# Moving every SBUF buffer behind the activation parts by 352 bytes in a hybrid attention layer

## The chip, the cores and the metric

The kernel runs on one core of a Trainium2 chip. The metric is the device time of the program in microseconds. The engines are named as in the profile: PE is TensorE's matmul stream and PEld its weight loads, DVE is VectorE, ACT is ScalarE, POOL is GpSimd, SP is SyncE, which issues nearly all DMAs.

## What is computed

One decoder layer on a sequence of 256 tokens with 4096 channels, in float32:

```python
h = rms_norm(x, pre_norm_w)
proj = h @ w_in                       # 4096 x 15408: queries, keys, values, gates
oa = nsa_mixer(...)                   # 16 heads: compressed, selected and window branches
ob = dilated_mixer(...)               # 16 heads: three (window, dilation) patterns merged
mix = concat([oa * silu(za), ob * silu(zb)])
x = x + rms_norm(mix @ w_out, post_norm_w)   # w_out: 4096 x 4096
```

Nearly all of the arithmetic is in the two large products with `w_in` and `w_out`. Attention over 256 tokens is small beside them.

## The kernel before, in words

**Precision.** A float32 product is made from three single-pass products. Each operand is split into a high part, which is the value rounded to the format that TensorE reads in one pass (fp32r), and a low part, which is the rest. The kernel sums hi·hi, hi·lo and lo·hi.

**Chunks and pairs.** The weights are worked through in 38 chunks of 512 columns by the helper `gemm_pair` (and one chunk of the compression weights and a narrow one of gate columns, which are handled apart at L810 and L821). A chunk has 32 blocks of 128 rows, taken two at a time as 16 pairs. For a pair, SP brings 128 x 2 x 512 float32 values into one of four slots of `raw` (`load_pair`, L384). ACT writes the high part to `w_parts[:, 0]` (`split`, L929), DVE subtracts it from `raw` and writes the low part to `w_parts[:, 1]` (L1239). PE then runs 12 matmuls: for each of the two row blocks and each of the two token tiles, L640 (stationary activation hi, moving weight hi), L643 (activation hi, weight lo) and L646 (activation lo, weight hi). The stationary operand is 128 columns of `x_parts` (512 bytes in each partition); the moving operand is 512 columns of `w_parts` (2048 bytes). The count is 38 x 16 x 12 = 7296 such matmuls, the last chunk's held pairs among them.

**Order.** Each engine's program is written out by hand. Attention, rotations, softmax and transposes are placed at fixed steps between the pairs of the large products, so that PE always has a pair ready. The semaphores `hi_ready`, `lo_ready` and `weights_used` tie ACT, DVE, PE and SP together through four slots.

**Placement in SBUF.** `build` has a bump allocator: `at` is the next free byte offset in each partition, `sb` rounds sizes up to 32 bytes, and a buffer may be given an explicit `offset` to share bytes with an earlier one. Such offsets are all worked out from buffers of the same list (`region`, `late`, `v_off` and so on). The first buffer is `x_parts` (65536 bytes a partition), the activation parts. All others come behind it. Worked out from the list, the byte offsets that matter are:

| buffer | role in the matmuls | offset before | modulo 64 | offset after | modulo 64 |
|---|---|---|---|---|---|
| x_parts | stationary of L640, L643, L646; moving of L810 | 1152 | 0 | 1152 | 0 |
| raw | landing place of weight DMAs | 99456 | 0 | 99808 | 32 |
| w_parts | moving of L640, L643, L646, L821 | 115840 | 0 | 116192 | 32 |
| b_q_hi, b_k_hi | L674 stationary, moving | 164992, 152704 | 0 | +352 | 32 |
| b_pt_hi | moving of L689, L691 | 181376 | 0 | +352 | 32 |
| vc (also b_v_hi) | stationary of L718, L689, L690 | 213536 | 32 | 213888 | 0 |
| w2_sb | stationary of L853 | 214560 | 32 | 214912 | 0 |
| pc_t (also b_pt_lo) | moving of L718, L690 | 215584 | 32 | 215936 | 0 |

Blocks and slots inside these buffers step by multiples of 512 bytes, so one remainder holds for all of a buffer. `x_parts`, `w_parts` and nearly all large buffers start at 1152 modulo 2048 before the change.

Of the kernel before, what the change touches and what calls it, by code (L numbers as in the profile page):

```python
# [111 lines left out]
def build(nc, x, x_t, positions, norm_cols, consts, w_in, w1, w2, post_w, w_out, out):  # L112

    ctx = ExitStack()
    with ctx:
        at = [1152]

        def sb(name, shape, dt=F32, offset=None):
            size = 4 * math.prod(shape[1:])
            where = at[0] if offset is None else offset  # L120
            if offset is None:
                at[0] += (size + 31) // 32 * 32
            t = nc.alloc_sbuf_tensor_at(name, shape, dt, offset=where)
            return t, where
# [2 lines left out]
        x_parts, _ = sb("x_parts", [P, KB, 2, SEQ], F32R)  # L127
        x_hi, x_lo = x_parts[:, :, 0, :], x_parts[:, :, 1, :]

        mix_t, region = sb("mix_t", [P, KB, SEQ])  # L130
        xt_raw, _ = sb("xt_raw", [P, KB, SEQ], offset=region)
        flat, _ = sb("flat", [P, CMP_LEN, 2, 2, GROUPS * CMP_PAD], F32R, offset=region)
# [1689 lines left out]
```

## Time and profile before

| | |
|---|---|
| Median of 2 runs | 1766.16 us (1765.94 and 1766.38) |
| Span of the profiled execution | 1763.9 us, first to last instruction; its own device time is not listed apart, the two runs' times stand 2.0 to 2.5 us above this span |
| PE busy | 1757.8 us, 7902 matmul records |
| PE weight loads | 1456.4 us |
| DVE, ACT, POOL busy | 1153.4, 886.8, 598.9 us |
| DMA | 344.77 MB, mean 195 GB/s |

Matmuls are pipelined: a record lasts some 0.39 us, but the next one starts about 0.23 us after it. So the busy time of PE is a union of overlapping records, and what counts for the pace is the distance from start to start, which is read from the order in time. Rows of that view give starts in us with two decimals.

### The profile page before, as it was taken

The page shows a single profiled execution, that of the slowest core. Times are in us where ns is not written, and L with a number is a line of the kernel's source. Part 1 is how long each engine was busy: PE and PEld are TensorE (multiplying, and loading weights), DVE is VectorE, ACT ScalarE, POOL GpSimd, SP SyncE. Part 2 cuts the span into 40 slices and gives each one's busy share as a digit, 9 for nine tenths or more (in the row PEclk, how much of TensorE's full clock was granted, in tenths as well). Part 3 has the DMA queues.
Part 4 walks back from the last instruction along what each step waited for, and adds up shares of the span by engine and source line. Part 5 has one row for each costly group of instructions (what it writes and reads, how often), then busy time and mean ns, then how long its engine had stood idle before and what let it go on. Part 6 is the DMA issues. An engine that isn't in the chain of part 4 may idle for free.

```text
span 1763.9 us, 22877 instructions
## 1 busy us (share of the span) xinstructions
PE 1757.8 (100%) x7902; PEld 1456.4 (83%) x7902; DVE 1153.4 (65%) x1192; ACT 886.8 (50%) x1216; POOL 598.9 (34%) x834
## 2 busy tenths in 40 slices
PE   9999999999999999999999999999999999999998
PEld 7888888888888888888888888888888888888886
DVE  7657656787888878656665666566655784444445
ACT  7643455464554545456435643564456554444443
POOL 3335303367593948721353034304431510000000
PEclk9999999999999999999999999999999999999999
DMA  9866687656565656666666666666666656667665
GB/s 294 254 199 188 188 248 229 179 161 185 157 189 151 185 160 174 183 197 182 179 195 196 182 181 197 194 190 176 191 194 191 190 185 217 213 213 212 213 202 204
DMA packets 184267, 344.77 MB, mean 195 GB/s; under 512 B 15216, under 2 KB 19568, under 8 KB 184176
## 3 DMA queue, kind: packets, MB, share of 16 engines
q1 hardware_dynamic: 183456, 342.58, 66.2%
q8 instruction: 62, 1.02, 0.2%
q10 hardware_dynamic: 720, 0.93, 0.1%
q14 instruction: 29, 0.24, 0.0%
HBM read 339.27 MB, written 4.19 MB: 195 GB/s over the span
## 4 chain that ended last, share of the span: by engine, by line
PE 99%; DMA 0%; ACT 0%; SPq 0%; DVE 0%; ACTq 0%; issue 0%
PE acc L640 31%; PE acc L646 31%; PE acc L643 31%; PE acc L821 1%; PE scores L810 0%; PE scores L709 0%; DMA raw<-in_w_in 0%; PE scores L742 0%; PE scores L741 0%; PE scores L740 0%; PE heads L757 0%; PE heads L758 0%; PE heads L759 0%; PE scores L665 0%; PE heads L692 0%; PE trans L657 0%
## 5 line engine op out<-in xcount | busy, mean ns | idle before, releaser
L1239 DVE TENSOR_TENSOR w_parts<-raw,w_parts 128x1024 fp32r<-128x1024 f32 x620 | 784.4, 1266 | 556.9 <-ACT w_parts L929 555.3
L929 ACT ACTIVATE w_parts<-raw 128x1024 fp32r<-128x1024 f32 x620 | 656.2, 1059 | 662.6 <-PE acc L646 649.6
L640 PE MATMUL acc<-w_parts,x_parts 128*128 128x512 f32 x2424 | 946.7, 391 | 0.2 <-DVE w_parts L1239 0.2
L646 PE MATMUL acc<-w_parts,x_parts 128*128 128x512 f32 x2424 | 943.8, 389 | 0.0
L643 PE MATMUL acc<-w_parts,x_parts 128*128 128x512 f32 x2424 | 943.3, 389 | 0.0
L646 PEld LDWEIGHTS acc<-w_parts,x_parts 128*128 128x128 f32 x2424 | 455.1, 188 | 95.8 <-DVE x_parts L1281 0.3
L640 PEld LDWEIGHTS acc<-w_parts,x_parts 128*128 128x128 f32 x2424 | 455.3, 188 | 93.4 <-issue 0.6
L643 PEld LDWEIGHTS acc<-w_parts,x_parts 128*128 128x128 f32 x2424 | 455.3, 188 | 93.0
L515 POOL COPY rot<-tok_b 32x256 f32<-32x256 f32 x120 | 86.9, 724 | 140.6 <-DVE tok_b L1613 135.7
L499 POOL TENSOR_TENSOR rot<-tok_a,trig 128x512 f32<-128x512 f32 x18 | 30.6, 1699 | 260.5 <-ACT tok_a L935 121.4
L515 POOL COPY b_first_t<-probs 32x128 f32<-32x128 f32 x64 | 31.1, 485 | 163.1 <-DVE probs L1686 160.6
L1603 DVE RECIPROCAL mixed<-mixed 128x256 f32<-128x256 f32 x32 | 55.8, 1745 | 0.4
L515 POOL COPY b_later_t<-probs 32x256 f32<-32x256 f32 x64 | 49.2, 769 | 19.1 <-DVE probs L1686 16.6
L949 ACT ACTIVATE probs<-probs,negmax 128x128 f32<-128x128 f32 (+1 forms) x80 | 34.7, 435 | 32.0 <-DVE negmax L1480 32.0
L483 POOL TENSOR_TENSOR rot<-rot,tok_a 128x512 f32<-128x512 f32 x15 | 27.6, 1842 | 55.5 <-ACT tok_a L968 55.2
L515 POOL COPY rot<-probs 32x256 f32<-32x256 f32 x64 | 40.5, 632 | 17.3 <-DVE probs L1520 14.8
L581 POOL CAST pc_t<-rows_c 32x128 fp32r<-32x128 f32 x64 | 27.7, 432 | 32.9 <-DVE rows_c L1577 30.3
L515 POOL COPY tok_a<-probs_more 32x128 f32<-32x128 f32 x64 | 35.9, 560 | 2.7
L515 POOL COPY k_t<-tok_a 32x256 f32<-32x256 f32 x32 | 20.0, 624 | 43.7 <-DVE tok_a L1348 42.5
L515 POOL COPY tok_a<-probs 32x128 f32<-32x128 f32 x64 | 33.8, 527 | 2.7
L515 POOL COPY k_t<-rot 32x256 f32<-32x256 f32 x32 | 28.4, 888 | 17.5 <-DVE rot L1458 8.6
L515 POOL COPY qraw_t<-probs_more 32x128 f32<-32x128 f32 x64 | 31.8, 497 | 2.7
(240 smaller groups left out, 1010.1 us busy)
## 6 DMA issues: line engine op xcount, KB each, us to landing
raw<-in_w_in SPq DMA_DIRECT2D x478, 512.0 KB, 3.7
raw<-in_w_out SPq DMA_DIRECT2D x128, 512.0 KB, 4.3
raw<-in_w SPq DMA_DIRECT2D x16, 512.0 KB, 4.7
x_tok<-in_x SPq DMA_DIRECT2D x16, 256.0 KB, 5.3
xt_raw<-in_x_t SPq DMA_DIRECT2D x7, 512.0 KB, 6.2
wpost<-in_post_w SPq DMA_DIRECT2D x8, 256.0 KB, 5.1
out<-y SPq DMA_DIRECT2D x3, 512.0 KB, 2.8
out<-y SPq DMA_DIRECT2D x5, 256.0 KB, 2.1
```

The costliest lines, as they stand in the source:

```text
L483: nc.gpsimd.tensor_tensor(square_sum, square_sum, squares[n % 2], ALU.add).then_inc(squares_added, 1)
L499: nc.gpsimd.tensor_tensor(r4, s4, cos, ALU.mult).then_inc(rope_muls, 1)
L515: last = nc.gpsimd.tensor_copy(dst[cols, :, :, rows], src[rows, :, :, cols])
L581: last = nc.gpsimd.tensor_copy(pc_t[cols, :, :, b * QUARTER // PART_ROWS, rows], src[rows, :, :, cols])
L640: nc.tensor.matmul(o, stat_hi, mov_hi, start=(k == 0), stop=False)
L643: nc.tensor.matmul(o, stat_hi, mov_lo, start=False, stop=False)
L646: last = nc.tensor.matmul(o, stat_lo, mov_hi, start=False, stop=(k == KB - 1))
L821: last = nc.tensor.matmul(acc[:, 1, v, :], flat[:, k, v, :, :], w_parts[:, :, at % SPLIT_SLOTS, k % 2, CMP_HIDDEN * v:CMP_HIDDEN * (v + 1) ...
L929: nc.scalar.activation(w_hi[:, n % SPLIT_SLOTS, :, 0:width], raw[:, n % RAW_SLOTS, :, 0:width], ACT.Copy).then_inc(hi_ready, 1)
L949: last = nc.scalar.activation(p, p, ACT.Exp, bias=negmax[:, slot % 4, i:i + 1], accum_out=den[:, slot % 4, i:i + 1])
L1239: V.tensor_tensor(w_lo[:, s, :, 0:width], raw[:, n % RAW_SLOTS, :, 0:width], w_hi[:, s, :, 0:width].bitcast(F32), ALU.subtract).then_inc(l ...
L1603: V.reciprocal(half, half).then_inc(silu_step, 1)
```

## The change

One line is added in `build`, behind the allocation of `x_parts` and ahead of all others:

```diff
         x_parts, _ = sb("x_parts", [P, KB, 2, SEQ], F32R)
         x_hi, x_lo = x_parts[:, :, 0, :], x_parts[:, :, 1, :]
 
+        at[0] += 352
         mix_t, region = sb("mix_t", [P, KB, SEQ])
         xt_raw, _ = sb("xt_raw", [P, KB, SEQ], offset=region)
```

`x_parts` stays at 1152. Every later buffer, those with explicit offsets included, moves up by 352 bytes = 5 x 64 + 32 in each partition. Nothing overlaps that did not before, and the list still ends inside SBUF. No instruction, wait, shape or order differs. Between two buffers behind `x_parts` the distance stays as it was; between `x_parts` and any other it grows by 352.

## Rows read from the trace of the kernel before

**Rows 1.** The page: span, busy time by engine, granted clock, DMA queue.
```profile
span 1763.9 us, 22877 instructions
PE 1757.8 (100%) x7902; PEld 1456.4 (83%) x7902; DVE 1153.4 (65%) x1192; ACT 886.8 (50%) x1216; POOL 598.9 (34%) x834
...
PEclk9999999999999999999999999999999999999999
...
q1 hardware_dynamic: 183456, 342.58, 66.2%
```

**Rows 2.** The page: the chain that ended last, by engine.
```profile
PE 99%; DMA 0%; ACT 0%; SPq 0%; DVE 0%; ACTq 0%; issue 0%
```

**Rows 3.** Waits of PE: line, releaser, us in total, times, longest.
```profile
PE scores L777 <- DVE stat L1317: 1.2, 1, 1.2
PE acc L640 <- DVE w_parts L1239: 0.2, 1, 0.2
```

**Rows 4.** The page's costliest groups: the split and the three products.
```profile
L1239 DVE TENSOR_TENSOR w_parts<-raw,w_parts 128x1024 fp32r<-128x1024 f32 x620 | 784.4, 1266 | 556.9 <-ACT w_parts L929 555.3
L929 ACT ACTIVATE w_parts<-raw 128x1024 fp32r<-128x1024 f32 x620 | 656.2, 1059 | 662.6 <-PE acc L646 649.6
...
L640 PEld LDWEIGHTS acc<-w_parts,x_parts 128*128 128x128 f32 x2424 | 455.3, 188 | 93.4 <-issue 0.6
```

**Rows 5.** Order in time, PE, 1420 to 1464 us: start, us, instruction; first and last.
```profile
1419.74 0.39 PE L646 MATMUL acc<-w_parts,x_parts 128*128 128x512 f32 x1
...
1463.94 0.39 PE L646 MATMUL acc<-w_parts,x_parts 128*128 128x512 f32 x1
```

**Rows 6.** Order in time, PE, the last product records and those after them.
```profile
1753.85 1.88 PE L908 MATMUL heads<-x_tok,cst 128*128 128x512 f32 x4
1755.56 1.02 PE L908 MATMUL scores<-x_tok,cst 128*128 128x512 f32 x2
```

**Rows 7.** Order in time, PE, around the first L718.
```profile
374.22 0.39 PE L643 MATMUL acc<-w_parts,x_parts 128*128 128x512 f32 x1
374.45 0.40 PE L646 MATMUL acc<-w_parts,x_parts 128*128 128x512 f32 x1
374.69 0.63 PE L718 MATMUL heads<-pc_t,vc 128*128 128x256 f32 x4
375.16 0.39 PE L640 MATMUL acc<-w_parts,x_parts 128*128 128x512 f32 x1
```

**Rows 8.** Order in time, PE, around the first L689.
```profile
863.69 0.40 PE L646 MATMUL acc<-w_parts,x_parts 128*128 128x512 f32 x1
863.93 0.28 PE L689 MATMUL heads<-b_pt_hi,b_v_hi 128*128 128x256 f32 x1
```

**Rows 9.** Order in time, PE, L853.
```profile
312.09 0.40 PE L646 MATMUL acc<-w_parts,x_parts 128*128 128x512 f32 x1
312.33 0.55 PE L853 MATMUL trans<-gelu,w_sb 128*128 128x64 f32 x4
```

**Rows 10.** Order in time, PE, around L674 to L676.
```profile
829.57 0.39 PE L646 MATMUL acc<-w_parts,x_parts 128*128 128x512 f32 x1
829.80 0.28 PE L674 MATMUL scores<-b_k_hi,b_q_hi 128*128 128x256 f32 x1
829.91 0.28 PE L675 MATMUL scores<-b_k_lo,b_q_hi 128*128 128x256 f32 x1
830.03 0.28 PE L676 MATMUL scores<-b_k_hi,b_q_lo 128*128 128x256 f32 x1
...
830.51 0.40 PE L640 MATMUL acc<-w_parts,x_parts 128*128 128x512 f32 x1
...
831.90 0.39 PE L640 MATMUL acc<-w_parts,x_parts 128*128 128x512 f32 x1
```

**Rows 11.** Stretches: PE, PEld, DVE, ACT, POOL busy; PEclk, DMA share, GB/s.
```profile
0.00:50.00 50.00, 48.59 (x205) 39.51 (x206) 37.01 (x48) 35.01 (x53) 15.99 (x13) 1.00 0.90 294
1420.00:1750.00 330.00, 330.00 (x1458) 273.34 (x1457) 170.45 (x161) 143.15 (x165) 7.22 (x8) 1.00 0.66 205
```

**Rows 12.** Waits of SP's queue: line, releaser, us in total, times, longest.
```profile
SPq L384 <- DVE w_parts L1239: 1248.0, 554, 5.1
```

## The prediction

> **What bounds the kernel.** I read the page first. PE is busy over the whole span at the full clock (2.4 GHz), the other engines are busy 65% of it or less, and the weight queue takes 66% of the DMA engines' time [rows 1]. The chain that ended last is PE for 99% [rows 2]. Then the waits of PE: 1.2 us at the very start and 0.2 us for a split, nothing else [rows 3]. So the kernel is one unbroken string of matmuls, and its time is their number times the distance between their starts. That distance comes from the order in time: in a stretch with nothing but the three products there are 195 distances between 1419.74 and 1463.94, 44.20 us, so 226.7 ns each [rows 5]. All but a few per cent of the time is this: 7296 x 0.2267 = 1654 us of the 1764.
>
> **What is inside 226.7 ns.** 512 columns at 2.4 GHz are 213.3 ns, or 512 periods; 226.7 ns are 544. So 32 periods (13.3 ns) are lost at each matmul. They aren't the plain cost of one matmul after another: the L908 records, which take two periods for each of 512 columns, follow each other at (1755.56 - 1753.85) / 4 = 427.5 ns, that is 1026 periods for 1024 [rows 6]. A weight load is running beside each product, recorded at 188 ns [rows 4]. I read the loss as the two reads of PE, 512 bytes of stationary and 2048 of moving operand in each partition, getting in each other's way or in step with something, at the addresses of the two. Those addresses are all that the change touches.
>
> **The change, part by part.** No instruction is added, dropped or moved, and no wait. Three things could respond to an address.
>
> (a) The products. 7296 matmuls (L640, L643, L646) and the 32 of L810 have one operand in `x_parts` and one behind it: 7328 whose two starts were equal modulo 64 before and differ by 32 after. All others keep their relation, both operands being moved. No row shows the new relation in a long string, so I bound it. The nearest rows are places where a product at the usual pace is followed by a matmul whose stationary operand starts at 32 modulo 64 while the moving one is at 0. L646 to L718 takes 374.69 - 374.45 = 0.24 us, L646 to L689 0.24, L646 to L853 0.24 [rows 7, 8, 9]; over the four L718 and eight L689 blocks it is 0.237. The control has all operands at 0 modulo 64: L646 to L674 takes 0.23 us [rows 10]. So the first distance at the new relation is longer by 10 ns. If it stayed so, 7328 x 10 ns = +73 us. That is the upper end. The control also shows how the pace behaves once it is disturbed: the six distances after the L674 block sum to 831.90 - 830.51 = 1.39 us, 231.7 ns each, before 226.7 comes back [rows 10]. A string that never settles would cost 5 ns a matmul, +37 us.
>
> The lower end: with the loss gone, a matmul would take 512 periods and the 2 of L908, 214.2 ns, -12.5 ns each and -92 us. I don't expect all of that, since nothing in the trace at 512 columns comes near it. The moving operand at 32 modulo 64 is seen only in L718 and L690, with 256 columns: four L718 in 375.16 - 374.69 = 0.47 us, 117.5 ns each [rows 7], where the aligned L674 to L676 take 0.12 (829.91 to 830.03) [rows 10]. That is no penalty for the moving operand's own offset, and 2.5 ns in its favour. It speaks against me; but there both operands are at 32, so their relation is the old one.
>
> The value that I take: the settled paces are whole multiples of 16 periods, 544 = 34 x 16 for 512 columns [rows 5] and 288 = 18 x 16 for 256 columns (0.12 us) [rows 10]. The pace seems to lock to such a step. One step more is 560 periods, 233.3 ns, which lies between 231.7 and 237. So +6.7 ns x 7328 = **+48.9 us**.
>
> (b) The splits and the small work. ACT's and DVE's halves of a split, 1059 and 1266 ns [rows 4], read and write at 32 modulo 64 instead of 0. A pair lasts 12 x 226.7 = 2720 ns on PE, and DVE is busy 52% of the long stretch [rows 11]. I price this at nothing: PE hides it, and DVE's split could last 2.1 times as long before PE waited. If that cover were gone, each ns over 2720 would count 620 times.
>
> (c) The DMAs. 183,456 packets of the weight queue land at another remainder. SP's queue waits 1248 us for slots to come free [rows 12], so it is early nearly everywhere. The exception is the start, where the DMA share is 0.90 and PE already loses 1.4 us of 50 [rows 11]. A few per cent more for each packet would cost up to 50 x 0.04 = 2 us there; I take 0. Between the ends (nothing, 2 us) the long stretch is nearer, with a share of 0.66 [rows 11].
> The Trainium skill (DMA: Bandwidth & Descriptors, "How a descriptor splits into AXI transactions") speaks against the change here: a descriptor that starts off a 256-byte boundary pays for the bytes below its start. By that, an estimate for 2048 bytes in beats of 32: from 128 modulo 256 before 68 beats, from 224 after 71, or 4% more. No row shows it; the sum would be the 2 us higher.
>
> **Sum.** 1766.2 + 48.9 + 0 + 0 = **1815 us**. The sum is made against the profiled execution (span 1763.9, so 1812.8 after); the runs stand 2.0 to 2.5 us above that span, and I add to their median.
>
> **Rivals.**
> *Same pace (1766 us).* The relation of the two addresses doesn't matter, or the stream settles to 544 periods again after a few disturbed matmuls, as it does after every disturbance in the trace [rows 10]. For it: the return to 226.7 is complete each time. Against it: the three 0.24 distances [rows 7, 8, 9] need a reason, and the stationary operand's own remainder would be one; that doesn't change for the products. 27%.
> The Trainium skill (SBUF — State Buffer, "Who interferes with whom") gives this result: PE has two independent read ports and never waits for anyone. The trace agrees with its companion number only in part: the page TensorE: Matmul & The Clock Gate ("Back-to-back issue gap") has 512 columns at about 216 ns, and here it is 226.7.
>
> *Faster (about 1717 us).* The mechanism sits in PE's reads during the weight load, at every product: with the starts 32 bytes apart the two reads stay clear of each other more of the time, and the lock falls one step lower, to 528 periods, 220.0 ns. 7328 x -6.7 ns = -48.9 us, 1717. With the loss gone but for what the L908 rows leave it would be 1674. It decides the sign as soon as the settled distance is under 226.7, and passes 2% (35 us) at 4.8 ns, 221.9 ns. For it: the 32 lost periods, and the 2.5 ns at L718. Against it: the first distances at the new relation are longer, not shorter. 31%, 17 of it at 528 periods or just above, 14 lower than that.
>
> *Slower, as forecast.* 42%: 560 periods or a string that doesn't settle (1803 to 1816) 27%, up to the full 10 ns (1839) 13%, beyond it 2%.
>
> That the change doesn't do what it says is no case: all offsets go through one counter.
>
> **How the numbers follow.** 2% is about what a measurement of this kernel can tell from no change. The forecast is the likeliest case, 1815, whose own range is 1800 to 1840. The case of no change and the faster one hold more than half together, so the range takes them in: down to 1705, which leaves out the 14% of a pace below 220 ns for the most part, and up to 1842, which leaves out 2%. Slower by over 2% (above 1801) 0.41, within 2% 0.28, faster 0.31.
>
> **What would show it.** In the changed kernel's order in time, the distance between two products over a long string: 233 ns if right, 226.7 for no change, 220 or less for the faster case. L674 to L676, whose operands both moved, should stay at 0.12 us. L646 to L718, whose stationary operand comes to 0 modulo 64 while the moving one goes to 32, should lie near the new pace. The waits of PE should stay under 3 us; if they grow instead, (b) or (c) was wrong. The DMA share should stay near 0.66 for the same bytes in each us. I am wrong at (a), the taken value, if the string settles on the other side, and wrong on the premise if the pace is 226.7 throughout.

## The result: slower by 2.7%

The changed kernel takes 1813.39 us (1813.30 and 1813.48) where the one before takes 1766.16; the ratio is 1.0268 with a 95% interval of 1.0250 to 1.0286. The profiled execution has a span of 1811.2 us, 47.3 more than before [rows 1].

In the changed kernel all line numbers behind the new line are one higher: L641, L644 and L647 are the three products that were L640, L643 and L646. Its page: span, busy time, the products' groups and the weight loads'.

```profile
span 1811.2 us, 22877 instructions
PE 1805.3 (100%) x7902; PEld 1456.9 (80%) x7902; DVE 1150.3 (64%) x1192; ACT 888.3 (49%) x1216; POOL 588.4 (32%) x834
...
PEclk9999999999999999999999999999999999999999
...
q1 hardware_dynamic: 183456, 342.58, 64.6%
...
L1240 DVE TENSOR_TENSOR w_parts<-raw,w_parts 128x1024 fp32r<-128x1024 f32 x620 | 780.7, 1260 | 605.4 <-ACT w_parts L930 603.5
...
L647 PE MATMUL acc<-w_parts,x_parts 128*128 128x512 f32 x2424 | 960.1, 396 | 0.0
L644 PE MATMUL acc<-w_parts,x_parts 128*128 128x512 f32 x2424 | 958.3, 395 | 0.0
L641 PE MATMUL acc<-w_parts,x_parts 128*128 128x512 f32 x2424 | 957.0, 395 | 0.0
L644 PEld LDWEIGHTS acc<-w_parts,x_parts 128*128 128x128 f32 x2424 | 455.2, 188 | 110.8
```

As many matmuls at the same full clock. A weight load still lasts 188 ns and a DVE split even 6 ns less than before [rows 4]; only the product records are longer, 395 or 396 ns where the page before has 389 to 391. PE's one wait, and the wait of SP's queue for free slots:

```profile
PE scores L778 <- DVE stat L1318: 1.2, 1, 1.2
```

```profile
SPq L385 <- DVE w_parts L1240: 1290.8, 556, 5.2
```

PE waits for nothing new [rows 3], and SP waits 43 us longer for slots [rows 12], as is to be expected where PE frees them later. The stretch at the start and a long one near the end, columns as in [rows 11]:

```profile
0.00:50.00 50.00, 48.78 (x199) 39.22 (x200) 35.37 (x48) 34.60 (x53) 14.31 (x12) 1.00 0.89 288
1460.00:1790.00 330.00, 330.00 (x1416) 265.47 (x1415) 164.58 (x151) 140.75 (x160) 7.20 (x8) 1.00 0.66 203
```

A stretch of 330 us now holds 1416 matmul starts instead of 1458. The DMA share is 0.66 as before, and at the start 0.89 instead of 0.90. The order in time on PE shows where the time is:

```profile
1459.77 0.39 PE L644 MATMUL acc<-w_parts,x_parts 128*128 128x512 f32 x1
1460.00 0.40 PE L647 MATMUL acc<-w_parts,x_parts 128*128 128x512 f32 x1
1460.23 0.39 PE L641 MATMUL acc<-w_parts,x_parts 128*128 128x512 f32 x1
1460.46 0.39 PE L644 MATMUL acc<-w_parts,x_parts 128*128 128x512 f32 x1
1460.70 0.40 PE L647 MATMUL acc<-w_parts,x_parts 128*128 128x512 f32 x1
...
1503.87 0.39 PE L644 MATMUL acc<-w_parts,x_parts 128*128 128x512 f32 x1
```

189 distances in 1503.87 - 1459.77 = 44.10 us: 233.3 ns each, 560 periods, where it was 226.7 and 544 [rows 5]. They aren't even. In the trace's nanoseconds three of them repeat as 231, 231, 238, together 700 ns, or 1680 periods; before, every one in such a stretch was 226 or 227.

### The profile page after: what moved, and what is told of

It is laid out like the page before. It is cut to its first block, busy times and chain, and to the rows that moved or that the text cites. A ratio compares the mean times of both kernels' runs of the same rounds, so it can differ in the third digit from the quotient of the medians.

```text
span 1811.2 us, 22877 instructions
## 1 busy us (share of the span) xinstructions
PE 1805.3 (100%) x7902; PEld 1456.9 (80%) x7902; DVE 1150.3 (64%) x1192; ACT 888.3 (49%) x1216; POOL 588.4 (32%) x834
## 3 DMA queue, kind: packets, MB, share of 16 engines
q1 hardware_dynamic: 183456, 342.58, 64.6%
## 4 chain that ended last, share of the span: by engine, by line
PE 100%; ACT 0%; ACTq 0%; issue 0%; DVE 0%
PE acc L647 31%; PE acc L644 31%; PE acc L641 31%; PE acc L822 1%; PE scores L811 0%; PE scores L710 0%; PE scores L741 0%; PE heads L758 0%; PE scores L743 0%; PE scores L742 0%; PE heads L759 0%; PE heads L760 0%; PE scores L778 0%; PE scores L666 0%; PE heads L693 0%; PE trans L658 0%
## 5 line engine op out<-in xcount | busy, mean ns | idle before, releaser
L647 PE MATMUL acc<-w_parts,x_parts 128*128 128x512 f32 x2424 | 960.1, 396 | 0.0
L644 PE MATMUL acc<-w_parts,x_parts 128*128 128x512 f32 x2424 | 958.3, 395 | 0.0
L641 PE MATMUL acc<-w_parts,x_parts 128*128 128x512 f32 x2424 | 957.0, 395 | 0.0
L644 PEld LDWEIGHTS acc<-w_parts,x_parts 128*128 128x128 f32 x2424 | 455.2, 188 | 110.8
L641 PEld LDWEIGHTS acc<-w_parts,x_parts 128*128 128x128 f32 x2424 | 455.3, 188 | 108.8
L647 PEld LDWEIGHTS acc<-w_parts,x_parts 128*128 128x128 f32 x2424 | 455.0, 188 | 107.8
L551 POOL TENSOR_TENSOR rot<-qraw_t,turn_t 128x512 f32<-128x512 f32 x8 | 14.2, 1780 | 60.5 <-ACT qraw_t L942 60.5
```

What stands on the lines that cost most here:

```text
L641: nc.tensor.matmul(o, stat_hi, mov_hi, start=(k == 0), stop=False)
L644: nc.tensor.matmul(o, stat_hi, mov_lo, start=False, stop=False)
L647: last = nc.tensor.matmul(o, stat_lo, mov_hi, start=False, stop=(k == KB - 1))
```

## The experiments

In the table, the shift is the distance in bytes that is added between the starts of stationary and moving operand of the products (moving less stationary), and the periods are the mean distance of two starts in a long undisturbed stretch, in ns, times 2.4, which gives periods of the full clock. Where a kernel adds lines of its own, the products' line numbers move with them: L642, L645 and L648 are the three products in e4, e7, e8 and e12.

| kernel | shift | modulo 256 | us | ratio to before (95%) | periods a product |
|---|---|---|---|---|---|
| before | 0 | 0 | 1766.2 | | 544.0 |
| after | 352 | 96 | 1813.4 | 1.0268 (1.0250 to 1.0286) | 560.0 |
| e1_shift_64 | 64 | 64 | 1782.1 | 1.0090 (1.0061 to 1.0119) | 549.3 |
| e2_all_352 | 0 | 0 | 1766.4 | 1.0000 (0.9989 to 1.0011) | 544.0 |
| e3_stat_32 | 32, see below | 32 | 1811.9 | 1.0258 (1.0229 to 1.0288) | 560.0 |
| e4_wparts_352 | 352 | 96 | 1813.3 | 1.0267 (1.0237 to 1.0296) | 560.0 |
| e5_shift_128 | 128 | 128 | 1806.2 | 1.0229 (1.0185 to 1.0273) | 557.7 |
| e6_shift_96 | 96 | 96 | 1813.2 | 1.0268 (1.0224 to 1.0312) | 560.0 |
| e7_inner_16 | 16 | 16 | 1800.8 | 1.0198 (1.0154 to 1.0242) | 556.0 |
| e8_inner_4 | 4 | 4 | 1842.1 | 1.0432 (1.0387 to 1.0477) | 570.0 |
| e9_shift_256 | 256 | 0 | 1766.2 | 1.0000 (0.9988 to 1.0011) | 544.0 |
| e10_shift_192 | 192 | 192 | 1812.6 | 1.0263 (1.0234 to 1.0293) | 560.0 |

**Is it the relation of the two operands, or where the moving one lies?** Two kernels part these. One moves everything, the activation parts too, by the same 352 bytes:

```diff
-        at = [1152]
+        at = [1152 + 352]
```

> Everything moved by 352 bytes, the activation parts too, so that the relation of stationary and moving start is that of before and both are at 32 modulo 64. Theory R (the relation of the two starts sets the pace): 1766 us, 226.7 ns. Theory M (the moving operand's own remainder modulo 64 sets it): 1813 us, 233.3 ns on average. If both operands' remainders add: up to 1840 us.

1766.4 us. The order in time of this kernel is that of before:

```profile
1499.83 0.39 PE L646 MATMUL acc<-w_parts,x_parts 128*128 128x512 f32 x1
1500.06 0.39 PE L640 MATMUL acc<-w_parts,x_parts 128*128 128x512 f32 x1
...
1501.87 0.39 PE L646 MATMUL acc<-w_parts,x_parts 128*128 128x512 f32 x1
```

Nine distances in 2.04 us are 226.7 ns, with moving and stationary operand of the products at 32 modulo 64. Moving all buffers alike by these 352 bytes costs nothing. The other kernel moves the activation parts by 32 bytes and all others by 64:

```diff
-        at = [1152]
+        at = [1152 + 32]
...
+        at[0] += 32
         mix_t, region = sb("mix_t", [P, KB, SEQ])
```

> Only the activation parts moved, by 32 bytes; all others land at 0 modulo 64 (moved by 64). Theory R: the starts differ by 32 modulo 64, 1813 us. Theory M: 1766 us. The rows of before at L718, L689 and L853 (0.24 us where the stationary operand alone is at 32) speak for a slower pace here, 1800 to 1840 us; if those were only a first disturbance, 1766.

1811.9 us, with `w_parts` and `raw` still at 0 modulo 64. Its shift needs the arithmetic: the parts move by 32, the rest by 64, so moving less stationary grows by 32. The pace is 560 periods too, in another string. Four distances make up its round (about 231, 235, 233 and 234 ns), 1500.73 - 1499.80 = 0.93 us in these lines; in the trace's nanoseconds it is 933.3, or 2240 periods:

```profile
1499.80 0.40 PE L641 MATMUL acc<-w_parts,x_parts 128*128 128x512 f32 x1
...
1500.73 0.40 PE L644 MATMUL acc<-w_parts,x_parts 128*128 128x512 f32 x1
```

Theory R, the relation of the two starts, holds and theory M, the moving operand's own remainder, falls in both runs.

**Is PE alone in it?** `w_parts` alone goes to the new remainder. `raw`, into which the DMAs write, stays where it was; the buffers behind `w_parts` move by 384 bytes, which leaves their remainder modulo 64 (modulo 256 they move by 128):

```diff
+        at[0] += 352
         w_parts, _ = sb("w_parts", [P, 2, SPLIT_SLOTS, 2, NC], F32R)
+        at[0] += 32
```

> Only w_parts at 32 modulo 64 (moved by 352); raw, mix_t and all other buffers at 0. PE reads w_parts, ACT and DVE write it, no DMA touches it. Theories R and M, the reads of PE: 1813 us and the uneven string of 231, 231 and 238 ns. If the DMAs into raw or the other buffers had a part in the slowdown: less than that, down to 1766.

1813.3 us, all of the loss, in the string 231, 231, 238; nine distances in 2.10 us:

```profile
1499.79 0.39 PE L645 MATMUL acc<-w_parts,x_parts 128*128 128x512 f32 x1
...
1501.89 0.39 PE L645 MATMUL acc<-w_parts,x_parts 128*128 128x512 f32 x1
```

The landing place of the DMAs has no part in the loss, since `raw` didn't move. The buffers behind `w_parts` did, but the kernel with everything moved has them elsewhere too and loses nothing.

ACT and DVE write `w_parts` while PE reads the activation parts, so their writes stand at the same new distance, and no run here stops them. The trace of the changed kernel speaks against them. From 1470 to 1740 us every three successive distances sum to 699 or 700 ns, over 1158 starts, while DVE and ACT are busy for half of the time and less (164.58 and 140.75 of 330 us in the stretch above). A loss that came from their writes would be there during a split and gone between two.

**Which distances count as the same?** Each of these kernels changes only the number in the line that the change adds.

> Every buffer behind the activation parts moved by 64 bytes instead of 352. If only the starts modulo 64 count: distance 226.7 ns, 1766 us. If the two operands' distance in bytes counts beyond 64 (a period of 128 or more): a pace between 222 and 237 ns, 1730 to 1840 us. If the splits or DMAs were behind the slowdown through their remainder modulo 64: also 1766 us, so this run does not tell that one apart.

1782.1 us: neither as before nor as after. So the remainder modulo 64, on which the prediction rested, isn't the whole of it. The order in time of this kernel:

```profile
1499.67 0.39 PE L647 MATMUL acc<-w_parts,x_parts 128*128 128x512 f32 x1
...
1501.73 0.39 PE L647 MATMUL acc<-w_parts,x_parts 128*128 128x512 f32 x1
```

Nine distances in 2.06 us: three rounds of 686.7 ns or 1648 periods (226, 229, 232 ns).

> Every buffer behind the activation parts moved by 128 bytes. The run at 64 gave 1782 us, so the relation counts beyond 64 bytes. Period 128: 226.7 ns and 1766 us, as before. Period 256 or 512: another pace, 1740 to 1840 us.

> Moved by 96 bytes, which is 352 less two times 128. Period 128: 1813 us and the same string 231, 231, 238 ns as after the change. Period 256: also 1813, since 352 is 96 modulo 256. Period 512 or longer: another pace.

128 gives 1806.2 us, which excludes a period of 128 bytes. Its round is of seven matmuls, 1626.7 ns or 3904 periods; to two decimals:

```profile
1499.69 0.39 PE L647 MATMUL acc<-w_parts,x_parts 128*128 128x512 f32 x1
...
1501.31 0.39 PE L641 MATMUL acc<-w_parts,x_parts 128*128 128x512 f32 x1
```

96 gives the time of 352, 1813.2 us, down to the string 231, 231, 238.

> Every buffer behind the activation parts moved by 256 bytes. 96 and 352 gave the same time and the same string, 0, 64 and 128 three different ones. If the relation counts modulo 256: 226.7 ns and 1766 us. If it counts modulo 512, and 96 and 352 agree by accident: another pace, 1780 to 1815 us.

1766.2 us and even distances again, as these lines of the kernel moved by 256 bytes show (ten in 2.26 us):

```profile
1499.71 0.39 PE L647 MATMUL acc<-w_parts,x_parts 128*128 128x512 f32 x1
...
1501.97 0.39 PE L641 MATMUL acc<-w_parts,x_parts 128*128 128x512 f32 x1
```

0 and 256 agree, 96 and 352 agree, and 0, 64, 96 and 128 all differ. So the relation counts modulo 256 bytes, as far as these two pairs can show it.

> Moved by 192 bytes, the last multiple of 64 below 256 that is untried. If relation 0 is the best case: over 1775 us. If the loss falls off evenly on both sides of 0, as at 64 (1782 us): about 1782. A faster kernel than before (a pace under 226.7 ns) has a chance of 1 in 8.

1812.6 us, and in the long stretch near the end 560 periods at each single matmul. The loss isn't even on both sides of 0: 64 ahead costs 16 us, 64 behind (192) costs 46. None of the relations tried is faster than 0, which the kernel before has; so no run pointed to a version that beats both.

**Below 32 bytes.** The allocator rounds sizes up to 32 bytes, so `w_parts` was placed inside a buffer that is 64 bytes longer (`e` is 4 elements, then 1); the buffers behind it move by those 64 bytes:

```diff
-        w_parts, _ = sb("w_parts", [P, 2, SPLIT_SLOTS, 2, NC], F32R)
+        w_size = 2 * SPLIT_SLOTS * 2 * NC
+        w_room, _ = sb("w_parts", [P, w_size + 16], F32R)
+        w_parts = w_room[:, e:e + w_size].rearrange("p (a s k n) -> p a s k n", a=2, s=SPLIT_SLOTS, k=2)
```

> Only w_parts moved, by 16 bytes, inside a buffer made 64 bytes longer. If the pace falls with the relation step by step (0 bytes 226.7 ns, 32 or 96 bytes 233.3, 64 bytes 229): 227 to 233 ns, 1770 to 1813 us. If the start inside a 32-byte piece doesn't count: 1766 us. A relation that keeps the two reads apart could be faster: under 1750 us.

> Only w_parts moved, by 4 bytes, one element. If whole lines of 16 or 32 bytes are read and the start inside one doesn't count: 1766 us. If a start off the line costs one more line at each read: some periods a matmul more, 1770 to 1815 us.

1800.8 and 1842.1 us; the second lies above the range that was expected. One element off is the worst case measured: 570 periods a product. In these lines nine distances take 1501.81 - 1499.67 = 2.14 us, 237.8 ns each:

```profile
1499.67 0.40 PE L642 MATMUL acc<-w_parts,x_parts 128*128 128x512 f32 x1
1499.90 0.40 PE L645 MATMUL acc<-w_parts,x_parts 128*128 128x512 f32 x1
1500.14 0.40 PE L648 MATMUL acc<-w_parts,x_parts 128*128 128x512 f32 x1
...
1501.81 0.40 PE L642 MATMUL acc<-w_parts,x_parts 128*128 128x512 f32 x1
```

These two runs can't tell a cost of the relation from one of a start off a 16- or 32-byte boundary; a kernel with both operands off by 4 bytes would, and wasn't run. So the dependence modulo 256 rests on the relations that are multiples of 32.

**Does the loss follow the length of the weight load?** Half of the stationary columns are left out in 30 of 32 row blocks, so half of the tokens get the sums of two row blocks only (the stationary columns are tokens, not output channels as the expectation has it):

```diff
-                        o = acc[:, parity, t, 0:width]
-                        stat_hi, stat_lo = hi[:, k, t * P:(t + 1) * P], lo[:, k, t * P:(t + 1) * P]
+                        m = P if k in (0, KB - 1) else P // 2
+                        o = acc[0:m, parity, t, 0:width]
+                        stat_hi, stat_lo = hi[:, k, t * P:t * P + m], lo[:, k, t * P:t * P + m]
```

> The kernel before with stationary operands of 64 columns instead of 128 in 30 of 32 row blocks, which leaves half of the output channels' sums out; matmuls, moving operands and transfers stay. Theory R says that the 32 periods over 512 are lost while a weight load reads beside the product, so they go with its length: 6840 matmuls lose 16 periods (6.7 ns) less, 1720 us. Rival, that they are a fixed price of a matmul or a start on a grid: 1766 us.

> The same in the changed kernel. Theory R: the 48 periods lost on average go down to 24 in 6840 matmuls, 10 ns each, 1745 us, and the cost of the 352 bytes falls from 47 to about 25 us. If only the start decides, and the length of the load doesn't: the cost of the 352 bytes stays at 47 us.

Both kernels missed what was expected of them. The loads are shorter, as the weight loads of the first of the two show:

```profile
L644 PEld LDWEIGHTS acc<-w_parts,x_parts 128*64 128x64 f32 (+1 forms) x477 | 65.7, 138 | 43.1
```

138 ns instead of 188. But that kernel takes 1786.4 us (ratio 1.0115, 1.0085 to 1.0144), 20 us more than before, at 551.5 periods a product; with the 352 bytes it is 1798.3 us (1.0182, 1.0153 to 1.0212), 15 us less than the changed kernel, at 555.8. Half of the stationary columns made one faster and the other slower. So the loss over 512 periods is not an amount for each byte loaded, as theory R was put there. It isn't a fixed price either, since the rival's 1766 us is excluded as well. What the pair does show is that the cost of the 352 bytes falls from 47 us to 12 when the stationary operand has half of its columns. That shortens the load and also halves the rows of `acc` that a product writes; the operands' addresses, the moving operand and the number of matmuls stay. That it is the load's length which counts, and not the narrower output, is not shown.

## Why the prediction was right

**The bound.** PE's unbroken string was the bound and is the bound after; 1.2 us of waits in all.

**Term (a), the products: right in mechanism, 7% too large in size.** The mechanism was that the distance between the starts of the two operands sets the pace, and the runs show it. 560 periods was the value taken and is the settled pace to a tenth of a period. The term was 48.9 us for 7328 matmuls; the span grew by 47.3. The products' own share of that is smaller. In the trace before, the 7189 distances from one product to the next sum to 1634.9 us, 227.4 each and not 226.7, for the disturbed stretches are in them [rows 10]. After, they sum to 1680.5, so the step is 45.6 us or 6.3 ns. Of the some 3 us that the term was too large, 2.3 are in the 6.3 ns instead of 6.7 and 0.9 in the 139 matmuls of the term that aren't a product with another behind it. The rest of the span's growth is 1.6 us. The first product starts 0.4 us later (6.14 instead of 5.70 us; with everything moved it is 6.15, so this isn't the relation), and 1.2 came from the places between the products' runs, most of it from matmuls that I had put at nothing because both of their operands move. They pay when the uneven string runs into them. The first L758 block of the changed kernel shows it:

```profile
405.47 0.40 PE L758 MATMUL heads<-pt_hi,v_hi 128*128 128x512 f32 x1
405.70 0.40 PE L759 MATMUL heads<-pt_lo,v_hi 128*128 128x512 f32 x1
405.94 0.39 PE L760 MATMUL heads<-pt_hi,v_lo 128*128 128x512 f32 x1
406.17 0.39 PE L641 MATMUL acc<-w_parts,x_parts 128*128 128x512 f32 x1
```

0.70 us for three, where the same three took 0.68 in the trace before:

```profile
395.57 0.39 PE L757 MATMUL heads<-pt_hi,v_hi 128*128 128x512 f32 x1
...
396.25 0.39 PE L640 MATMUL acc<-w_parts,x_parts 128*128 128x512 f32 x1
```

Over all 24 such blocks it is 701.5 ns against 680.0.

**The remainder was the wrong one.** The prediction compared the starts modulo 64. The runs show 256. That the rows still gave the right answer was luck. The relation at L718, L689 and L853 before [rows 7, 8, 9] was not just any odd multiple of 32. Those buffers start at 32 modulo 256 and `w_parts` at 128, so the moving operand was 96 ahead, and 352 is 96 modulo 256. Had the change been 64 bytes, the argument by remainders modulo 64 would have said 1766 us, and the run gave 1782.

**The whole steps of 16 periods** held for whole rounds, not for one matmul at a time. In the long strings of the changed kernel no product takes 560 periods; three take 1680. Rounds of other kernels are whole multiples of 16 too: 1648 for three (64 bytes), 3904 for seven (128 bytes), 2240 for four (32 bytes) and 2224 for four (16 bytes: 227, 234, 235, 230 ns). So "one step more" was a guess that came out: the mean pace is 560 at 32, 96 and 192 bytes, but 549.3, 556.0, 557.7 and 570.0 at 64, 16, 128 and 4, none of which is a whole step. Why 16, no run shows.

**The bounds.** The upper end from the first disturbed distance, +10 ns, was not reached by this relation, though 4 bytes came to it (26 periods or 10.8 ns over 544). The lower end was far off: nothing tried came under 544.

**Terms (b) and (c)** are nothing, as priced: `w_parts` alone gives the whole loss, and the whole set moved by 352 gives none, with each split and each DMA landing at the new remainder. The estimate of 2 us more for the start of a descriptor off a 256-byte boundary, from the Trainium skill (DMA: Bandwidth & Descriptors, "How a descriptor splits into AXI transactions"), isn't borne out: the packets of the weight queue took 64.6% of 1811.2 us, 1170 us, where they took 66.2% of 1763.9 us, 1168 us [rows 1]. With everything moved by 352 it is 66.4% of 1764.4 us, 1172, and with `raw` unmoved (`w_parts` alone) 64.6% of 1811.3 us, 1170; the time with everything moved is 1766.4 us.

**The rival of the same pace** needed another reason for the three 0.24 distances, the stationary operand's own remainder. The result excludes the rival itself, since the activation parts didn't move and the pace changed, and the run with everything moved excludes its reason: the stationary operand is at 32 modulo 64 there, and the pace is 544. The Trainium skill (SBUF — State Buffer, "Who interferes with whom") has PE's two read ports independent and PE never waiting on anyone. The measurement decides against that rule in this form: with one instruction stream, the same work and no new wait of PE's, the distance between the two operands' addresses alone moves the time from 1766 to 1813 us. The 216 ns that the prediction took from the Trainium skill's page TensorE: Matmul & The Clock Gate ("Back-to-back issue gap") are that page's figure for a matmul by itself; for a sustained stream of loads and matmuls with 512 columns it has about 131 ns, and no long string here is faster than 226.7.

**The faster rival** was a real possibility by its mechanism and failed on a fact that no row held: relation 0 is the best of those tried.

**What was said to show it.** 233 ns in a long string: 233.3. L674 to L676 at 0.12 us: in the changed kernel

```profile
850.95 0.39 PE L647 MATMUL acc<-w_parts,x_parts 128*128 128x512 f32 x1
851.18 0.28 PE L675 MATMUL scores<-b_k_hi,b_q_hi 128*128 128x256 f32 x1
851.29 0.28 PE L676 MATMUL scores<-b_k_lo,b_q_hi 128*128 128x256 f32 x1
851.41 0.28 PE L677 MATMUL scores<-b_k_hi,b_q_lo 128*128 128x256 f32 x1
```

0.11 and 0.12. L646 to L718 near the new pace: 0.23 us. That is less than the 0.24 of before [rows 7], though both operands moved together here and their relation is still 96. Over the eight L690 blocks of the changed kernel (L689 before) the same kind of step runs from 231 to 238 ns at that one relation. So a single distance depends also on where in its round the string is hit, and one such row alone would have been a weak ground for the upper bound:

```profile
383.78 0.39 PE L647 MATMUL acc<-w_parts,x_parts 128*128 128x512 f32 x1
384.01 0.64 PE L719 MATMUL heads<-pc_t,vc 128*128 128x256 f32 x4
```

**What stays open** is how the two reads, if it is they, disturb each other; the runs show the distance of the addresses and not the reads. That the two reads meet in the same part of SBUF whenever their addresses agree in some way modulo 256 would fit the period, but the narrow loads don't fit a plain count of such meetings.

## What to carry to other kernels

A string of matmuls can have a pace of its own that no wait and no busy share shows: divide a long stretch by the number of starts and compare with the columns at the granted clock. Where a string like this one (fp32r operands, 512 moving columns and a load of 128 columns for each matmul) is the bound, keep the distance between the starts of stationary and moving operand at a multiple of 256 bytes, and look again at the pace after any buffer of an odd size has been put between them. To tell relation from place, move both together once.

## What the runs showed of the hardware that was not expected

- The distance between the addresses of the two operands counts modulo 256 bytes, and not evenly: 0 and 256 give 544 periods for 512 columns, 64 gives 549.3, 128 gives 557.7, 32, 96 and 192 give 560.
- The pace isn't a mean with scatter. With full loads and relations from 16 bytes up it locks into short rounds (of one, three, four or seven matmuls) that repeat through the whole 270 us looked at in each trace, and each of these is a whole multiple of 16 periods at 2.4 GHz. At 4 bytes a round takes 48 matmuls, 11,400 ns.
- Stationary operands of 64 columns instead of 128, with loads of 138 ns instead of 188, made the well-placed kernel slower by 20 us.
